# Residual additions of eight closing steps: two of four quarters moved from POOL to VectorE

## What is computed

```python
# first block
x = x + gate_m[:, None, :] * rms_norm(merged @ w_out[i], g_post_mix[i])
h = modulate(rms_norm(x, g_pre_ffn[i]), shift_f, scale_f)
u, gt = jnp.split(h @ w_ffn_in[i], 2, axis=-1)
f = (jax.nn.silu(u) * gt) @ w_ffn_out[i]
x = x + gate_f[:, None, :] * rms_norm(f, g_post_ffn[i])
...
# second block, for l in range(2)
h = ada_norm(x, norm_g[l, 0], mod[:, 0, 0], mod[:, 0, 1])
x = x + 0.5 * mod[:, 0, 2][:, None, :] * swiglu(h, ffn_w13[l, 0], ffn_w2[l, 0])
h = ada_norm(x, norm_g[l, 1], mod[:, 1, 0], mod[:, 1, 1])
x = x + mod[:, 1, 2][:, None, :] * token_mixer(h, ...)
h = ada_norm(x, norm_g[l, 2], mod[:, 2, 0], mod[:, 2, 1])
x = x + 0.5 * mod[:, 2, 2][:, None, :] * swiglu(h, ffn_w13[l, 1], ffn_w2[l, 1])
...
return rms_norm_2(x, final_g)
```

## Time and profile before

| | |
|---|---|
| median of 3 runs | 2177.31 us (2171.54 to 2182.89) |
| profiled execution, its own time | 2176.83 us |
| its span in the profile | 2175.0 us |
| granted TensorE clock, mean | 0.956 of full speed |
| busy: PE, DVE, ACT, POOL | 1987.5, 1015.2, 527.5, 258.1 us |
| the chain that ended last, by engine | PE 83%, DVE 5%, DMA 3%, issue 3%, ACT 3%, POOL 2% |

### The profile page before, as it was taken

The page is one execution under the profiler, slowest core; times in us unless marked ns, Lnnn a source line. Parts: engine busy times, 40 slices in busy tenths (PEclk is TensorE's granted clock), DMA queues, the critical chain, the costliest instruction groups (busy, mean ns, idle before and its releaser), DMA issues.

```text
span 2175.0 us, 28432 instructions
## 1 busy us (share of the span) xinstructions
PE 1987.5 (91%) x11760; PEld 1680.5 (77%) x11760; DVE 1015.2 (47%) x1821; ACT 527.5 (24%) x792; POOL 258.1 (12%) x294
## 2 busy tenths in 40 slices
PE   2999987787998999899999999999799999999997
PEld 2786777775877777689988666999799887658996
DVE  4464567766312345555431353554545421526553
ACT  1011210101102000243320233333433311324332
POOL 0211242332010000100011031000100010220000
PEclk9998899998999999999999899999899999899998
DMA  8764503304243788634424304442454323015441
GB/s 326 291 247 179 194 17 139 124 33 155 97 147 150 291 375 344 284 155 174 188 82 168 126 4 155 178 200 105 158 221 182 155 114 148 32 70 205 174 174 39
DMA packets 33501, 358.74 MB, mean 165 GB/s; under 512 B 3712, under 2 KB 4352, under 8 KB 8832
## 3 DMA queue, kind: packets, MB, share of 16 engines
q1 hardware_dynamic: 33408, 357.44, 42.2%
HBM read 356.38 MB, written 1.05 MB: 164 GB/s over the span
## 4 chain that ended last, share of the span: by engine, by line
PE 83%; DVE 5%; DMA 3%; issue 3%; ACT 3%; POOL 2%; SPq 0%; POOLq 0%; DVEq 0%; ACTq 0%
PE psum L889 11%; PE psum L841 8%; PE psum L842 8%; PE psum L843 8%; PE psum L795 6%; PE psum L853 4%; PE psum L917 4%; PE psum L854 4%; PE psum L855 4%; PE psum L806 3%; PE psum L907 3%; PE psum L757 3%; PE psum L1017 2%; PE psum L1166 2%; PE psum L1026 1%
## 5 line engine op out<-in xcount | busy, mean ns | idle before, releaser
L841 PE MATMUL psum<-split 128*128 128x256 f32 x1408 | 403.2, 286 | 17.9 <-POOL split L2085 17.9
L842 PE MATMUL psum<-split 128*128 128x256 f32 x1408 | 402.6, 286 | 0.0
L843 PE MATMUL psum<-split 128*128 128x256 f32 x1408 | 402.4, 286 | 0.0
L889 PE MATMUL psum<-hT,ring 128*128 128x256 f32 x1280 | 286.6, 384 | 7.0 <-DMA ring<-in_in 5.3
L841 PEld LDWEIGHTS psum<-split 128*128 128x128 f32 x1408 | 274.5, 195 | 20.0 <-issue 18.6
L889 PEld LDWEIGHTS psum<-hT,ring 128*128 128x128 f32 x1280 | 246.2, 193 | 42.7 <-DMA ring<-in_in 6.1
L842 PEld LDWEIGHTS psum<-split 128*128 128x128 f32 x1408 | 274.7, 195 | 1.4
L843 PEld LDWEIGHTS psum<-split 128*128 128x128 f32 x1408 | 274.3, 195 | 0.0
L1549 DVE TENSOR_TENSOR split<-ring,split 128x2048 fp32r<-128x2048 f32 x88 | 202.6, 2302 | 147.9 <-ACT split L1257 147.9
L1257 ACT ACTIVATE split<-ring 128x2048 fp32r<-128x2048 f32 x88 | 168.4, 1913 | 163.3 <-PE psum L843 163.3
L2018 POOL TENSOR_TENSOR x_res<-x_res,scratch 128x512 f32<-128x512 f32 x32 | 40.5, 1274 | 1098.1 <-DVE scratch L1629 827.0
(11 more groups left out here) (319 smaller groups left out, 2604.9 us busy)
## 6 DMA issues: line engine op xcount, KB each, us to landing
ring<-in_up SPq DMA_DIRECT2D x55, 2048.0 KB, 9.0
ring_down<-in_down SPq DMA_DIRECT2D x55, 1024.0 KB, 4.8
ring<-in_ada SPq DMA_DIRECT2D x22, 2048.0 KB, 7.8
ring<-in_in SPq DMA_DIRECT2D x19, 2048.0 KB, 8.8
arena<-in_ada SPq DMA_DIRECT2D x18, 2048.0 KB, 12.0
arena<-in_ada SPq DMA_DIRECT2D x32, 512.0 KB, 4.5
ring<-in_w_out SPq DMA_DIRECT2D x6, 2048.0 KB, 9.1
ring<-in_gates SPq DMA_DIRECT2D x4, 2048.0 KB, 7.7
```

The lines of the kernel that those rows point to most:

```text
L841: mm(dst, up_hi[:, h, a], h_hi[:, kt_], start=(kt_ == 0 and j % 2 == 0), stop=False, skip_group_check=True)
L842: mm(dst, up_hi[:, h, a], h_lo[:, kt_], start=False, stop=False, skip_group_check=True)
L843: last = mm(dst, up_lo[:, h, a], h_hi[:, kt_], start=False, stop=(kt_ == KD - 1), skip_group_check=True)
L889: last = mm(bank[4 + j % 2][:, 0:S], w[:, k * 512 + n * P:k * 512 + n * P + P], hT[:, k, :], start=(k == 0), stop=(k == KD - 1))
```

## The change

In each `finish`, DVE itself adds the second and the fourth quarter (i = 1 and 3 in the order) into `x`, right behind having scaled it. It first waits for its own scaling (`fin_read`) and for the addition of the quarter before (`x_ready` = 4n + i). `add` on POOL leaves these two out and keeps the first and the third.

```diff
--- before.py
+++ after.py
@@ -1628,6 +1628,11 @@
                     else:
                         last = tt(fin[:, i % 2], bank[j], r, ALU.mult)
                     last.then_inc(fin_read, 1)
+                    if i % 2:
+                        dve.wait_ge(fin_read, 4 * n + i + 1)
+                        dve.wait_ge(x_ready, 4 * n + i)
+                        dst = x[:, j // 2, (j % 2) * 512:(j % 2 + 1) * 512]
+                        tt(dst, dst, fin[:, i % 2], ALU.add).then_inc(x_ready, 1)
 
             def kk_norms(j):
 
@@ -2013,6 +2018,8 @@
             def add(n, order):
 
                 for i, j in enumerate(order):
+                    if i % 2:
+                        continue
                     pool.wait_ge(fin_read, 4 * n + i + 1)
                     dst = x[:, j // 2, (j % 2) * 512:(j % 2 + 1) * 512]
                     tt(dst, dst, fin[:, i % 2], ALU.add).then_inc(x_ready, 1)
```

## The result

| | before | after |
|---|---|---|
| median, us | 2176.03 (2167.84 to 2183.71) | 2167.43 (2161.21 to 2179.62) |
| ratio of times, 95% interval | | 0.9965 [0.995, 0.9979] |
| profiled execution, us | 2176.83 | 2170.16 |
| its span, us | 2175.0 | 2168.4 |

The change makes the kernel 8.6 us faster, 0.35%. The question is where four times the expected gain comes from.

The account below looks back on a forecast made before the run. PE, busy 91% of the span, was taken as the bound. Terms 4 x 0.20 + 2 x 0.58 + 2 x 0.07 = 2.1 us take the profiled execution from 2176.83 to 2174.7; the forecast median was 2175.2 us, range 2170.0 to 2181.0.

Parts of the forecast that it names:

- The price of the addition: Each new addition on DVE was taken to cost 0.69 us, with 0.65 and 1.27 as ends.
- 0.58 at the fourth quarter of n = 2, 4, 5, 7: The fourth square would start at 2164.68 instead of 2165.26 (times of n = 7), 0.58 us earlier.
- 0.65 at n = 3 and 6: Only DVE's own scaling counts there, so the fourth square would start 0.65 us earlier.
- the second quarter at nothing: Moving the second addition gains nothing, and delays the third scaling by only 0.00 to 0.05 us.
- the draw at n = 0 and 1: With all banks full, scaling and adding alternate on DVE; the last square comes only 0.07 us earlier.
- the fillers end 0.20 before `xn`: At n = 3 PE's filler matmuls hold back the transposes, so 0.20 of 0.65 us gets through.
- all of it at n = 4: PE waits again for the gate row there, on a chain that bypasses the transposes, so the whole 0.58 us arrives.
- A: Rival: the fillers don't matter, the full gain arrives everywhere, 3.8 us, giving 2173.5; chance 0.12.
- B: Rival: POOL's addition still holds DVE's after reporting its end, 0.74 us each; 6.0 us slower, 2183.3; chance 0.06.
- Its small form at n = 1: Part of rival B: POOL's MEMSET of 0.95 us, beginning with the fourth addition, blocks DVE; up to 0.9 us once.
- C: Rival: no effect, as the addition takes 1.27 on DVE too or unseen waits absorb the gains; 2177.3 us; chance 0.12.
- so 0.20 it stays: Behind the transposes at n = 3 one chain follows, so the 0.20 us persists; likewise at n = 2, 5 and 6.

Follow-up runs that it names:

- after, unchanged: The changed kernel timed once more without any edit, against the kernel before: 2164.62 us, ratio 0.9949 [0.9928, 0.997].
- both unchanged: Repeat timings without any edit: the kernel before, 2174.65 us (ratio 1.0 [0.9975, 1.0024]), and the changed kernel, 2164.62 us.

## Why the prediction was right and wrong

*Right.* The price of the addition (0.69 taken, 0.692 measured); 0.58 at the fourth quarter of n = 2, 4, 5, 7 (0.56 to 0.59) and 0.65 at n = 3 and 6 (0.62); the second quarter at nothing; the draw at n = 0 and 1; above all that the fillers end 0.20 before `xn`, so that about 0.26 of 0.6 gets through, and all of it at n = 4. Sum 2.3 against 2.1.

*The rivals.* A fell: at n = 2 to 6 the first transpose follows the last filler by 0.11. B fell: all 16 additions of DVE took 0.69. The eight that had only POOL's addition to wait for (both at n = 0 and 1, the fourth quarter at n = 2, 4, 5 and 7) began 0.10 behind its end, so nothing was held. Its small form at n = 1 fell too: POOL's MEMSET ran from 905.96 to 906.92, beside DVE's addition at 906.13, which still took 0.69. By the rule of the Trainium skill (SBUF — State Buffer, section "SBUF: two separate sides") a VectorE instruction with two SBUF inputs is locked out only by a GpSimd instruction that reads SBUF, and a memset reads none; the trace agrees. C fell with the price of 0.692 and the local gains of the table.

*What failed* is the step "so 0.20 it stays", with its "0.20 each of 0.58" for n = 2 and 5, and with it the sum: it takes for granted that each stage lasts as long as before once it starts earlier. It does not, in either direction. The sum of the local terms, 2.3, was right, and the 8.6 us are mostly another term, put at nothing without a reason: TensorE's time at the lower clock.

- Upwards: in after, unchanged, the mixers behind n = 2 and 5 took 201.3 instead of 204.6 us. Of the 3.3 us only 0.27 are the term; the missing term is 3.0 us at each of two places, the 6.8 us in which the clock no longer is at its lower level.
- Downwards: at n = 4 the network starts 0.59 earlier, and the stage takes 211.49 instead of 211.57 (both unchanged), so 0.51 are lost. Its first matmuls run at the lower clock in both, for 5.05 us from its start in before and for 5.70 in after; the 0.65 more are worth half, about 0.3. The other 0.2 stay open. At n = 3 0.26 became 0.09, with 0.26 us more at the lower clock.

After against before, both unchanged, by spans: 2171.8 - 2163.3 = 8.5 us, of which 1.7 lie ahead of n = 0 (no instruction there differs, and the part varies from 616 to 626 us among kernels that are the same there), 6.6 are the mixers and 0.2 the rest. The measured 8.6 us and the two 3.3 us agree as far as one execution of each can say; that the remaining 2 us are chance is not shown. Nor do the traces show what fixes the place of the falls. It was luck for the change that a shift of a few tenths fell on the good side: the same shift less one filler gave nothing.

The clock as such was in the page of before (0.956 on average), and the argument had no place for it: the range came from the local terms and the spread of a median, and no rival had a shift in it. One with "the mixers come 0.2 to 0.5 us earlier; their two low stretches, 20 us each, may get shorter or longer" would have put some 7 us on either side (an estimate from what was seen later: 3.3 us gained in each of two mixers, 7.6 lost in one).

## What to carry to other kernels

Where TensorE's clock goes down behind a thin stretch, as here in the mixers, the worth of a small local gain need not be its own size: make the table of stages with the time at the lower clock first, and let the range take in half of that time. Look at the thin stretches themselves, since 22 fillers in each mixer shortened it by 7.1 us, twice what the change did. One pair of profiles is not the change's account until a second profile of each has shown which differences repeat, and the mean clocks of the executions without a profile tell how common the profiled case is.

## What the runs showed of the hardware

- How long the clock stayed at its lower level went with tenths of a microsecond: the second low stretch of a mixer was 3.4, 10.2 or 27.3 us long in executions whose first fall stood between 90.8 and 91.3 us behind L889.
- Single waits of TensorE of at most 1.63 us stood in front of both falls; the engine was busy for 1.98 of 3.40 us ahead of the first and for 5.07 of 6.90 ahead of the second. With fillers in place of the waits both falls were gone from there, and one stretch of 3.4 us came 94.3 us behind L889.
- It repeats, up to a point: before gave 204.6 us for both mixers in both of its profiles, while the part ahead of n = 0 differed by 2.4 us; after gave 201.3 three times and 212.2 once.
- Handovers between DVE and POOL took 0.10 us towards DVE and 0.08 towards POOL, and none of DVE's additions lost anything to POOL's work beside it (0.691 to 0.693 us, all 16).
